# Key, query and pooling tiles of a retention and MoE step as block products

## The reference

```python
proj = einsum('btd,de->bte', rmsnorm(x), w_in)        # 1024 -> 44 tiles of 128 columns
q, k, v, g, p, ga, gb = split(proj)                   # 4, 4, 8, 8, 4, 8, 8 tiles
qh, kh = rotary(q, pos), rotary(k, pos) * 128 ** -0.5
o, S_new = retention(qh, kh, v, S0)                   # chunks of 128; S' = c S + k (x) v for a sample
ya = (silu(g) * groupnorm(o)) @ w_ret_branch
yb = (pool_w(multi_scale_mean(p) - p) * pool_scale) @ w_pool_branch
x = x + (sigmoid(ga) * ya + sigmoid(gb) * yb) @ w_out
x = x + moe(rmsnorm(x))                               # top 4 of 32 experts, clamped SwiGLU
```

## Time and profile before

| | us |
|---|---|
| three runs, median (lowest to highest) | 1185.95 (1185.29 to 1187.32) |
| the profiled execution's own time | 1186.07 |
| its span, first to last instruction | 1184.3 |
| TensorE busy | 1139.4 (96%) |
| VectorE busy | 376.3 (32%) |
| ScalarE busy | 169.0 (14%) |
| GpSimd busy | 57.3 (5%) |
| mean granted TensorE clock | 0.991 |
| transfers | 455.18 MB, mean 384 GB/s |

### The profile page before, as it was taken

The page is one execution under the profiler, slowest core; times in us unless marked ns, Lnnn a source line. Parts: engine busy times, 40 slices in busy tenths (PEclk is TensorE's granted clock), DMA queues, the critical chain, the costliest instruction groups (busy, mean ns, idle before and its releaser), DMA issues.

```text
span 1184.3 us, 14904 instructions
## 1 busy us (share of the span) xinstructions
PE 1139.4 (96%) x5835; PEld 578.0 (49%) x5835; DVE 376.3 (32%) x843; ACT 169.0 (14%) x376; POOL 57.3 (5%) x77
## 2 busy tenths in 40 slices
PE   9999999999999999999989999989999989999997
PEld 7889999984434334343333333333333333333432
DVE  4358874752122222221212121212121212121222
ACT  2121231030111111111101010101111111010112
POOL 3154110000000000000000000000000000000000
PEclk9999999999999999999999999999999999999999
DMA  9772789798999999999999999999999999999996
GB/s 321 229 241 72 249 270 386 251 367 329 419 426 431 425 428 430 432 424 434 422 430 431 429 430 434 421 431 429 437 424 430 424 430 430 434 425 432 425 421 244
DMA packets 66807, 455.18 MB, mean 384 GB/s; under 512 B 4321, under 2 KB 39597, under 8 KB 45760
## 3 DMA queue, kind: packets, MB, share of 16 engines
q1 hardware_dynamic: 64544, 447.99, 91.9%
q0 software_dynamic: 1872, 5.95, 1.5%
q10 hardware_dynamic: 344, 0.61, 0.1%
HBM read 448.65 MB, written 6.11 MB: 384 GB/s over the span
## 4 chain that ended last, share of the span: by engine, by line
PE 66%; DMA 31%; SPq 1%; DVE 1%; issue 0%; ACT 0%; DVEq 0%; ACTq 0%
PE psum L1326 23%; DMA ring<-in_w_down 23%; PE psum L1337 12%; PE psum L1096 10%; DMA ring<-in_w_gate_up 8%; PE psum L1236 7%; PE psum L1413 4%; PE psum L1393 1%; PE psum L1447 1%; PE psum L1123 1%; PE psum L1403 1%; SPq L676 1%; PE psum L1448 1%; PE psum L1422 1%; DMA consts<-in_consts 0%
## 5 line engine op out<-in xcount | busy, mean ns | idle before, releaser
L1326 PE MATMUL psum<-ring,x_T 128*64 128x512 f32 x1004 | 454.1, 598 | 9.2 <-DMA ring<-in_w_gate_up 8.5
L1327 PE MATMUL psum<-ring,x_T 128*64 128x512 f32 x994 | 449.0, 598 | 0.0
L1326 PEld LDWEIGHTS psum<-ring,x_T 128*64 128x64 f32 x1004 | 130.6, 137 | 273.5 <-issue 251.4
L1337 PE MATMUL psum<-ring,act_T 128*64 128x512 f32 x960 | 219.2, 610 | 24.0 <-DMA ring<-in_w_down 24.0
L1337 PEld LDWEIGHTS psum<-ring,act_T 128*64 128x64 f32 x960 | 70.8, 140 | 160.5 <-issue 141.8
L1327 PEld LDWEIGHTS psum<-ring,x_T 128*64 128x64 f32 x994 | 129.2, 137 | 0.0
L2375 DVE TENSOR_TENSOR h_raw<-psum,params 128x512 f32<-128x512 f32 x32 | 22.1, 692 | 299.4 <-PE psum L1393 299.4
L2392 DVE TENSOR_TENSOR z_T<-z_T,psum 128x264 f32<-128x264 f32 x112 | 43.0, 426 | 203.9 <-PE psum L1448 203.9
L1236 PE MATMUL psum<-ring 128*128 128x280 f32 (+1 forms) x384 | 92.0, 395 | 0.6 <-issue 0.6
L1236 PEld LDWEIGHTS psum<-ring 128*128 128x128 f32 x384 | 71.6, 190 | 15.5 <-issue 1.0
L1413 PE MATMUL psum<-normed,one_hot 128*128 128x512 f32 x168 | 74.4, 592 | 0.0
(11 more groups left out here) (322 smaller groups left out, 940.5 us busy)
## 6 DMA issues: line engine op xcount, KB each, us to landing
ring<-in_w_gate_up SPq DMA_DIRECT2D x32, 4096.0 KB, 31.7
ring<-in_w_gate_up SPq DMA_DIRECT2D x59, 2048.0 KB, 28.4
ring<-in_w_down SPq DMA_DIRECT2D x56, 2048.0 KB, 33.4
ring<-in_w_in SPq DMA_DIRECT2D x21, 1024.0 KB, 6.5
ring<-in_w_down SPq DMA_DIRECT2D x12, 1024.0 KB, 27.9
spare<-in_w_gate_up SPq DMA_DIRECT2D x5, 1280.0 KB, 36.7
ring<-in_state_ret POOLq DMA_DIRECT2D x8, 512.0 KB, 7.5
ring<-v_rows SPq DMA_DIRECT2D x8, 512.0 KB, 7.1
```

What stands on the lines that cost most here:

```text
L1326: mm(psum[0:CAP, 2 * j + n], x, gate, start=first, stop=final)
L1327: last = mm(psum[CAP:P, 2 * j + n], x, up, start=first, stop=final)
L1337: last = mm(psum[j * CAP:(j + 1) * CAP, 4 + n], hidden[:, j, 4 * h + i], w, start=h == 0 and i == 0, stop=h == 1 and i == 3)
```

## The change

The twelve key, query and pooling tiles become six groups of seven block products, numbered 0 to 5, ahead of the gate groups, which are now 6 to 17 (GATE_FROM = 6). A half is 140 tokens there (280 / 2, for queries too) and 132 in the gates. The sums of token blocks are made for 140 before the first group and remade for 132 between group 5 and 6. The buffers of the weight sums differ by group; more_sums for groups 0 to 2 is done beside the value tiles, for 3 to 6 in groups 0, 2, 3 and 4. The chunks of these groups are given back by product 4. ScalarE copies the turned keys out (it was VectorE) and does the rank-one products, as four scaled copies of one head each (it was GpSimd). The scores are computed behind the last pair instead of between pooling tiles.

The core of the diff:

```diff
+_aux(K0 + 1, ("hist",), (6,))
 for _j in range(4):
-    _aux(_j + 10, ("k", _j), (4 + _j % 2,))
-_aux(15, ("s_meta",), (4, 5, 6, 7))
-_aux(17, ("score", 0), (4,))
-_aux(18, ("score", 1), (5,))
-_aux(19, ("s_next", 0), (6, 7))
+    _aux(K0 + 4 + _j // 2 * 2, ("k", _j), (6 - _j % 2 * 2,))
+_aux(K0 + 9, ("s_meta",), (4, 5, 6, 7))
+_aux(K0 + 10, ("s_next", 0), (6, 7))
+_aux(K0 + 11, ("score", 0), (4,))
+_aux(K0 + 11, ("score", 1), (6,))
-GATES = (N_IN - G0) // 2
+GATE_FROM, GATES = (G0 - K0) // 2, (N_IN - K0) // 2
+SUMS_BEFORE = {4: 0, 5: 2, 6: 1, **{g: g - 2 for g in range(GATE_FROM + 3, GATES)}, ...}
+RANK_ONE_AT = {1: (0,), 2: (1,), 3: (2,), 4: (3, 4), 5: (5,), 6: (6, 7)}
 # group_of_chunk: the chunks of the new groups are given back by product 4
-    if kind == "in" and c >= G0:
-        return (c - G0) // 2
+    if kind == "in" and c >= K0:
+        return (c - K0) // 2
 # TensorE
+            def early_groups():
+                for g in range(GATE_FROM):
+                    product(g, 1)
+                    product(g, 2)
+                    if g > 0:
+                        product(g - 1, 3)
+                    if g < GATE_FROM - 1:
+                        for a in AUX_AFTER[K0 + 2 * g]:
+                            aux(a)
+                    product(g, 6)
+                    product(g, 7)
+                    if g > 0:
+                        product(g - 1, 4)
+                    if g == GATE_FROM - 1:
+                        aux(("s_next", 0))
+                    product(g, 5)
+                    if g < GATE_FROM - 1:
+                        for a in AUX_AFTER[K0 + 2 * g + 1]:
+                            aux(a)
+                g = GATE_FROM - 1
+                aux(("score", 0))
+                product(g, 3)
+                aux(("score", 1))
+                product(g, 4)
 # ScalarE
+            def rank_one(b):
+                act_e.wait_ge(pool_step, 1)
+                act_e.wait_ge(spread_in[b % 4], 16 * (b // 4 + 1))
+                for h in range(H):
+                    last = A(spread_v[:, b % 4, h], spread_v[:, b % 4, h], ACT.Copy, scale=k_cols[:, h, b:b + 1])
+                last.then_inc(rank_one_ready, 1)
+            def take_early_groups():
+                for g in range(GATE_FROM):
+                    keep_part(g, 1)
+                    if g > 0:
+                        take_early_sum(g - 1)
+                    keep_part(g, 6)
+                    if g > 0:
+                        take_early(g - 1, 0)
+                    if g in (2, 3):
+                        for j in range(2 * g - 4, 2 * g - 2):
+                            take_turned(j)
+                    if g > 0:
+                        take_early(g - 1, 1)
+                    keep_part(g, 5)
 # ScalarE, gate groups
                     keep_part(g, 5)
-                    if g > 0:
+                    if g > GATE_FROM:
                         take_quarters(g - 1)
+                    for b in RANK_ONE_AT.get(g - GATE_FROM, ()):
+                        rank_one(b)
 # VectorE
+            def early_groups():
+                for g in range(GATE_FROM):
+                    if g >= 2:
+                        rope(K0 + 2 * g - 3)
+                    if g == 0:
+                        aux(("v", 7))
+                    if g == GATE_FROM - 1:
+                        aux(("s_meta",))
+                    finish_first(g)
+                    if g != 1 and g < GATE_FROM - 1:
+                        more_sums({0: 3, 2: 4, 3: 5, 4: 6}[g])
+                    if g > 0:
+                        finish_second(g - 1)
+                    if 0 < g < GATE_FROM - 1:
+                        rope(K0 + 2 * g - 2)
+                    finish_third(g)
+                    if g == 0:
+                        aux(("hist",))
+                g = GATE_FROM - 1
+                aux(("s_next", 0))
+                aux(("score", 0))
+                finish_second(g)
```

More of the change, by code:

```diff
@@ L1090, in product @@
                     pe.wait_ge(w_more_ready, 2 * g + 2)
-                    bank, a, b = total, sums[:, 2], x[:, high, second]
+                    bank, a, b = total, sums[2], x[:, high, second]
                 else:
                     pe.wait_ge(quarter_ready, QUARTER_AT[g, 22])
-                    bank, a, b = extra, w[:, high, P:2 * P], x_sums[:, 2]
+                    if g == GATE_FROM:
+                        pe.wait_ge(x_sums_ready, 8)
+                    bank, a, b = extra, w[:, high, P:2 * P], xs[:, 2]
                 for k in range(HK):
-                    last = mm(psum[:, bank, 0:HALF], a[:, k], b[:, k], start=k == 0 and i in (1, 2, 7),
+                    last = mm(psum[:, bank, 0:h], a[:, k], b[:, k], start=k == 0 and i in (1, 2, 7),
                               stop=k == HK - 1, skip_group_check=i not in (1, 2, 7))
@@ L1181, in turn_roots @@
                 pe.transpose(psum[:, 3, 384:384 + 28], rows[0:28, 0:P], ident[0:28, 0:28]).then_inc(params_turned, 1)
-            for n in (*range(G0), *range(N_IN, T_YA)):
+            for n in (*range(K0), *range(N_IN, T_YA)):
                 if n == T_POOL:
+                    early_groups()
                     gate_groups()
@@ L1690, in take_quarters, with take_early_sum, take_early @@
                 A(out[:, 1], out[:, 1], f).then_inc(gates_taken, 1)
+            def take_early_sum(g):
+                h = half_of(g)
+                act_e.wait_ge(product_done, PRODUCT_AT[g, 3])
+                nc.scalar.copy(group_gates(g)[:, 0, h:2 * h], psum[:, SUM_BANK[g % 2], 0:h]).then_inc(c12_taken, 1)
+            def take_early(g, s):
+                n, out = K0 + 2 * g + s, group_gates(g)
+                if s == 0:
+                    act_e.wait_ge(c12_taken, g + 1)
+                    act_e.wait_ge(quarter_ready, QUARTER_AT[g, 11])
+                else:
+                    act_e.wait_ge(quarter_ready, QUARTER_AT[g, 22])
+                    act_e.wait_ge(quarter_ready, QUARTER_AT[g, 21])
+                if n < P0:
+                    if n >= K0 + 2:
+                        act_e.wait_ge(roped, n - K0 - 1)
+                    w = NA if n < Q0 else NT
+                    nc.scalar.copy(rope_y[0:64, s, 0:w], out[64:128, s, 0:w])
+                    last = nc.scalar.copy(rope_y[64:128, s, 0:w], out[0:64, s, 0:w])
+                else:
+                    p = n - P0
+                    nc.scalar.copy(p_ext[:, p, 0:NM], out[:, s, NT:NA])
+                    nc.scalar.copy(p_s[:, p], out[:, s, NPR:NT])
+                    last = nc.scalar.copy(p_ext[:, p, NM:], out[:, s, 0:NPR])
+                last.then_inc(act_took, 1)
@@ new lines, in rope @@
+            def rope(n):
+                j, s = n - K0, n % 2
+                dve.wait_ge(act_took, took_count(n))
+                if j == 0:
+                    dve.wait_ge(consts_in, 32)
+                scale = DK ** -0.5 if j < H else 1.0
+                w = NA if j < H else NT
+                x, y = group_gates(j // 2)[:, s, 0:w], rope_y[:, s, 0:w]
+                step(V.scalar_tensor_tensor(x, x, scale, const("cos")[:, 0:w], ALU.mult, ALU.mult))
+                step(V.scalar_tensor_tensor(y, y, scale, const("sin")[:, 0:w], ALU.mult, ALU.mult))
+                step.wait()
+                if j < H:
+                    V.tensor_tensor(k_T[:, j], x, y, ALU.add).then_inc(roped, 1)
+                    return
+                h = j - H
+                if h == 0:
+                    dve.wait_ge(few_cleared, 2)
+                own = q_only[:, h].rearrange("p b c -> p (b c)")[:, 0:33 * NS - 32:33]
+                step(V.tensor_tensor(own, x[:, NPR:NT], y[:, NPR:NT], ALU.add))
+                V.tensor_tensor(q_T[:, h], x[:, 0:NT], y[:, 0:NT], ALU.add).then_inc(roped, 1)
@@ L2023, in gate_groups @@
+            def gate_groups():
+                gate_x_sums()
+                aux(("score", 1))
+                for g in range(GATE_FROM, GATES):
                     finish_first(g)
@@ L2102, in branch_groups @@
                 for part in (1, 2, 3):
[L2103 removed]
+                    sum_of_halves(gate_a, out_diff, 3, part)
             few = NS + NM
```

292 lines of the change are left out of this document (147 added, 145 removed).

## The result

| | us |
|---|---|
| changed kernel, median of four runs (lowest to highest) | 1198.61 (1198.0 to 1199.88) |
| kernel before, median of four runs (lowest to highest) | 1185.62 (1185.12 to 1187.32) |
| ratio, with its 95% interval | 1.0108 (1.0091 to 1.0126) |
| profiled execution, its own time and its span | 1199.12 and 1197.3 |

A forecast was written before the change was run, and what follows sets the result against it. TensorE was taken to bound the kernel until the experts start, everything behind shifting one to one; -4.4 + 3.9 + 1.0 + 0.5 + 4.7 + 1.7 = +7.4 on 1186.07 gave 1193.4 us, range 1185 to 1197.

The forecast's parts named there:

- Term 1: Key, query and pooling stage on TensorE: 42 block products at 0.953 us replace 44.40 us of tiles, -4.4 us.
- Term 2: Early stage: TensorE pauses because VectorE's sums wait for weight chunks, plus two short waits; +3.9 us, from 1.9 to 7.
- 0.8 before (2,3): TensorE's pause before product 3 of pair 2, behind sums needing chunk 8, which was taken to land after 6.3 us.
- the rival of the later chunks: Early stage: chunks 8 and 9 both take 11.3 us and the clock falls there; 1197 us, chance 0.11 with dearer products.
- dearer products: Block products at 125 ns an instruction, not 119.2, add 1.9 us; chance 0.11 together with the rival of the later chunks.
- row 7: Gate stage: ScalarE waits for this value row's broadcast, holding TensorE before product 6 of group 7; +4.7 us (4.2 to 5.2).
- the 1.9 before (3,3): TensorE's pause of 1.9 us before product 3 of pair 3, behind sums that wait for chunk 9.
- The meta state: Early stage: it waits for a quarter behind the sums of pair 6, 0.3 us.
- the second score: Moved to the end of the early stage, it waits for the bank VectorE empties of the state product, 0.5 us.
- Row 0 in gate group 1: ScalarE's scaled copies delay its copy of the next group's part 1, which TensorE's product 6 needs; +1.0 us (0.5 to 2.4).
- Rows 3 and 4: Gate group 4: both rows' scaled copies on ScalarE make the copy ready at 137.5 against 137.1; +0.5 us.
- The clock behind it: Behind the pause for row 7, TensorE's granted clock at 0.61 then 0.96 loses +1.7 us, or 0 if it stays.

The follow-up runs named there:

- later states: Changed kernel with GpSimd's loads of states 4 to 7 issued behind the copy of the key columns, 21 us later; 1194.67 us (1.0072).
- The kernel with both parts together: Changed kernel with VectorE's sums one group before use, rank-one rows 0 and 1 in group 2 and row 7 in group 7; 1184.3 us (0.9985).
- all products on GpSimd: Changed kernel with all eight rank-one products back on GpSimd, four ahead of the pooling and four behind it; 1196.7 us (1.0090).
- the experiment: Changed kernel with row 7 of the rank-one products made by ScalarE in gate group 7 in place of 6; 1190.81 us (1.0043).
- matmuls at the start: Changed kernel with five more matmuls of 8 columns at the start, ten more instructions ahead of the expert loop; 1206.66 us (1.0173).
- later sums: Changed kernel with VectorE's weight-block sums for pairs 4, 5 and 6 made one group before use in place of two; 1192.4 us (1.0054).
- later rows: Changed kernel with the four broadcast rows issued behind chunk 9 in place of chunk 8; 1197.79 us (1.0100).
- the repeated split kernel: Changed kernel with sums one group before use, rank-one rows 0 to 3 on ScalarE from group 2, 4 to 7 on GpSimd; measured again, 1183.99 us (0.9977).

## Why the prediction was right in sign and too low

**Term 1, -4.4 us: right.** 0.955 us a product against 0.953.

**Term 2, +3.9: measured +6.4 (the early stage lost 1.97 where -0.5 was predicted); this step failed in size.** The prediction let chunk 8 land after 6.3 us and paused 0.8 before (2,3) (its 54.4 and 6.3 make 60.7, not 60.9, so 0.6). It landed after 8.8, and (2,3) began 3.16 us late. The row with the states and rows in flight (11.3) was nearer than the empty one, and later states showed that it is the states, not the rows, that hold this chunk. This is the rival of the later chunks, which had the lower clock and 1197 us, and a chance of 0.11 together with dearer products. Then the step's second fault: the clock was lower behind this pause, 1.8 us over the next product, the transposes and product 6 (1.42, 1.28 and 1.64 us where full speed gives 0.95, 0.66 and 0.95). That was in the prediction only for row 7 and in a rival. In return the 1.9 before (3,3) did not come: TensorE was already 4.9 us late when chunk 9 landed. The meta state waited 1.0 (0.3 predicted), the second score 0.4 (0.5). 3.16 + 1.78 + 1.0 + 0.42 = 6.4.

**Row 0 in gate group 1, +1.0: measured +2.55** (0.58 in group 1, 1.97 in group 2), just beyond its range of 0.5 to 2.4. ScalarE's own timeline:

```profile
111.57 0.30 ACT L1713 ACTIVATE small<-small,consts 128x4 f32<-128x4 f32 x1 [2.40 <-DVE small L2058]
111.88 1.28 ACT L1735 ACT_TABLE_LOAD   x1
...
117.00 0.42 ACT L1744 ACTIVATE z_T<-z_T 128x264 f32<-128x264 f32 x1 [1.65 <-DVE z_T L2112]
117.34 1.69 ACT L1790 ACTIVATE ring<-ring 128x256 f32<-128x256 f32 x4
118.93 0.24 ACT L1727 COPY z_T<-psum 128x132 f32<-128x132 f32 x1
```

Row 0's product is one cause; the other is VectorE, late with the statistics that ScalarE's second root waits for. The kernel with both parts together parts them: with row 0 out of the group, 1.36 of the 2.55 go and 1.19 stay. With all products on GpSimd 0.95 stay (6.87 and 8.40 us for the two groups). The prediction gave this lateness "some tenths". Its sources on VectorE, the sums of x behind the last product and block sums of 1.0 us beside GpSimd's pooling, were named, but their effect was not followed through the root.

**Rows 3 and 4, +0.5: measured +0.6.** Right. The price of the four scaled copies was 1.69, not 1.5.

**Row 7, +4.7: measured +5.0.** Right, mechanism and place: the broadcast was issued at 153.00 and took 7.1 us; the experiment took the whole loss away by one number.

**The clock behind it, +1.7: measured +2.8; this step failed in size too.** The prediction took over the price of one row, behind a pause of 2.5 us: 0.61 and 0.96 over 8 us. Here it was 0.50 and 0.77. This pause was twice as long, but its length does not explain the price. With the wait for row 7 in place, other kernels lost 1.5, 1.9, 2.2 and 2.8 us behind pauses of 4.97, 5.13, 4.80 and 4.29 (first matmuls at the start, later sums, later states, later rows), and in the early stage pauses of 1.97 to 3.16 us cost 1.5 to 3.0. So one row could not give this term to better than about a microsecond, and what sets it within these bounds stays open.

**The sum.** Past the prediction: 0.4 at the start (not in it, and no more than scatter: the kernels with nothing added at the start begin this stage at 42.7 to 43.6 us), 2.5 of term 2, 1.55 of row 0, 0.1, 0.3, and 1.1 of the clock, 5.9 in all; 0.3 came back behind the mixer. That is 5.6 between the profiled executions; the median of the changed kernel is 0.5 below its profiled one, which leaves 5.2. The terms were low almost without exception, and what went the other way, the pause before (3,3) that did not come, is hidden in term 2. The range of term 2 held no lower clock. Against the changed kernel, the one-to-one shift behind the mixer held to 0.7 us in every kernel with 32 instruction packets but one (the repeated split kernel, 1.5).

## What to carry to other kernels

Before work with its own wait (a chunk of weights, a broadcast) is moved into an engine's queue, look at what is queued behind it: here one dictionary entry cost 7.8 us and another order of sums 6.2, and neither engine was busy. Make prefetch-like work as late as its use allows, when the queue is shared with work that is on the path. A pause on the engine that sets the end can be dearer than its length: add the slow stretch behind it, here 1.5 to 3.0 us for pauses of 2.0 to 5.1, as a range and not as one number, since it did not follow the length.

## What the hardware showed beyond that

- The granted clock: behind single idle stretches of TensorE of 1.97 to 3.16 us in the early stage it fell, and 1.5 to 3.0 us of work were lost; behind 4.29 to 5.13 us in gate group 7, 1.5 to 2.9. Nearly equal pauses (2.99 and 3.05) cost 1.8 and 3.0, and the longest of all (5.13) 1.9. A pause of 1.7 us in gate group 2 cost nothing in any kernel that has it. The pause of group 7 with TensorE kept at matmuls whose result nobody reads cost none either.
- Ten TensorE instructions more ahead of a loop (twice) or twenty (once) raised the instruction transfers from 32 to 59 packets (of 16 KB), and the expert stage lost 4.3, 4.4 and 4.6 us, with idle time that nothing in the profile ends. With the number kept there were 32, and it lost 0.7. An experiment that adds instructions should be read by stage, and this queue looked at first.
- Ten matmul instructions of 8 columns took 2.0 us at the start (4.81 to 6.80), 0.2 each; the twelve of 128 columns ahead of them took 0.23 each (2.09 to 4.81).

```profile
4.81 2.14 PE L1205 MATMUL psum<-ring 128*128 128x8 f32 x10
```
